# Decode-step kernel on one Trainium2 core: the prompt's latent attention gets its mask, identity and second queries one stage sooner, and the latent stage's last query stores are issued inside the attention

## What is computed

```
q_lat = einsum('bshd,chd->bshc', q[..., :QK_NOPE], w_uk)
def block(args):                                  # mla_prompt
    s = (einsum('bqhc,bkc->bhqk', ql, ckv) + einsum('bqhr,bkr->bhqk', qr, krope)) * MLA_SCALE
    p, _ = masked_softmax_stats(s, kpos[None, :] <= qpos[:, None])
    return einsum('bhqk,bkc->bqhc', p, ckv)
```

## Time and profile before

| what | value |
|---|---|
| median of three runs | 2103.25 us |
| profiled execution, first to last instruction | 2103.7 us |
| PE busy | 1934.1 us, 92% |
| DVE, ACT, POOL busy | 52%, 44%, 20% |
| latent stage and attention | about 638 to 1222 us of the span |
| the place of the change | 755 to 810 us of the span |

### The profile page before, as it was taken

How to read it: one execution, slowest core, us unless ns; L and a number is a source line. 1 busy time by engine, 2 the same in 40 slices (tenths; PEclk the granted TensorE clock), 3 DMA queues, 4 the chain that set the end, 5 groups by cost and what they waited for, 6 DMA issues and landing times. The chain is left out here.

```text
span 2103.7 us, 47545 instructions
## 1 busy us (share of the span) xinstructions
PE 1934.1 (92%) x17532; PEld 1475.6 (70%) x17532; DVE 1090.2 (52%) x3211; ACT 930.4 (44%) x2106; POOL 423.2 (20%) x583
## 2 busy tenths in 40 slices
PE   6999999788878968999999979999999989999997
PEld 5888888465656756676667746666666668888886
DVE  4423333377794437666767745555555753332232
ACT  4333332478772225556555534444444553333332
POOL 0111111234462213013310132222222210000000
PEclk9999999899999979999999989999999999999999
DMA  8333332443446451011200169977776462332231
GB/s 289 99 113 110 110 117 79 124 143 108 131 138 179 146 151 51 24 37 32 73 18 25 42 185 284 270 224 222 215 222 212 144 215 91 94 104 81 90 103 47
DMA packets 178428, 270.39 MB, mean 129 GB/s; under 512 B 28088, under 2 KB 138632, under 8 KB 169336
## 3 DMA queue, kind: packets, MB, share of 16 engines
q1 hardware_dynamic: 158456, 169.74, 28.5%
q0 software_dynamic: 19808, 98.40, 13.9%
HBM read 213.06 MB, written 54.76 MB: 127 GB/s over the span
## 5 line engine op out<-in xcount | busy, mean ns | idle before, releaser
L75 PE MATMUL proj_acc<-proj_w_hi,proj_x_hi 128*128 128x512 f32 (+2 forms) x544 | 197.5, 363 | 18.3 <-DVE proj_x_lo L299 12.6
L76 PE MATMUL proj_acc<-proj_w_lo,proj_x_hi 128*128 128x512 f32 (+2 forms) x544 | 196.0, 360 | 0.0
L77 PE MATMUL proj_acc<-proj_w_hi,proj_x_lo 128*128 128x512 f32 (+2 forms) x544 | 195.6, 360 | 0.0
L1614 ACT ACTIVATE mla_probs<-mla_probs,mla_bias 128x256 f32<-128x256 f32 (+15 forms) x128 | 152.6, 1196 | 22.3 <-DVEq L1678 13.2
L1671 DVE CUSTOM_DVE_ANT_0 mla_probs<-mla_scores,mla_zero 128x512 f32<-128x512 f32 x192 | 124.6, 686 | 64.8 <-PE mla_scores L1533 64.7
L1624 ACT ACTIVATE prompt_q_nope<-mla_turned 128x512 f32<-128x512 f32 x144 | 79.8, 597 | 163.7 <-PE mla_turned L1560 163.6
L1575 PE MATMUL mla_outs<-prompt_q_nope,prompt_val 128*64 128x256 f32 (+1 forms) x1152 | 136.2, 376 | 5.3 <-DVE prompt_q_nope L1688 3.9
L75 PEld LDWEIGHTS proj_acc<-proj_w_hi,proj_x_hi 128*128 128x128 f32 x544 | 104.0, 191 | 31.5 <-DVE proj_x_lo L299 12.6
L817 ACT ACTIVATE win_probs<-win_probs,win_bias 128x256 f32<-128x256 f32 (+1 forms) x256 | 117.4, 462 | 17.2 <-DVE win_bias L856 16.7
L1997 PE MATMUL dec_scores<-dec_keysT,sample_q_lat 128*64 128x512 f32 x512 | 123.0, 601 | 2.2 <-DVE dec_krT L2163 1.2
L353 DVE COPY proj_featT<-proj_tr 128x512 f32<-128x512 f32 x34 | 23.5, 692 | 188.1 <-PE proj_tr L406 186.4
(11 more groups left out here) (402 smaller groups left out, 4845.8 us busy)
## 6 DMA issues: line engine op xcount, KB each, us to landing
win_v_tile<-wv_out SPq DMA_DIRECT2D x75, 128.0 KB
proj_x_raw<-in_xT SPq DMA_DIRECT2D x17, 512.0 KB, 3.9
proj_rows<-in_x SPq DMA_DIRECT2D x17, 512.0 KB, 5.3
featT<-proj_featT POOLq DMA_DIRECT2D x34, 256.0 KB, 2.8
late_ckv<-in_xT SPq DMA_DIRECT2D x17, 512.0 KB, 6.8
host_buf<-mix SPq DMA_DIRECT2D x17, 512.0 KB, 3.6
late_ckv<-in_x SPq DMA_DIRECT2D x17, 512.0 KB, 4.1
y_out<-host_buf POOLq DMA_DIRECT2D x17, 512.0 KB, 6.5
```

Source lines behind the costliest of these rows:

```text
L75: pe.matmul(out, lh, rh, start=start, stop=False)
L76: pe.matmul(out, lh, rl, start=False, stop=False)
L77: return pe.matmul(out, ll, rh, start=False, stop=stop)
L1614: act.activation(row, row, ACT.Exp, bias=bias[:, at:at + 1], scale=-1.0, accum_out=total[:, at:at + 1]).then_inc(exp_done, 1)
```

## The change

Four edits. In the last chunk of the latent stage SP loads four more pieces ahead of the key store: the mask (256 KB, into the columns of `host_buf` that key chunk 3 will take later), the two parts of unit 1's queries, and the identity. After that store SP leaves the stage; the last stores of `q_rope` and `q_nope` are issued by SP inside the attention, `q_nope` between the loads of units 2 and 3, `q_rope` between key chunks 2 and 3. POOL copies the mask from `host_buf` to `mla_mask`, once, ahead of its first split. `probsT` lies in the memory of `k_nope` and its first write waits for `k_stored`.

```diff
@@ prompt_latent_projections, SP, last chunk
                     sp.dma_start(host.qr_raw[:, 0, :], io["mla_qr"][0:P, 0:host.CW]).then_inc(host.first_loaded, 16)
+                    sp.dma_start(host.mask_ahead, io["mla_mask"]).then_inc(host.mask_loaded, 16)
+                    sp.dma_start(host.qn_raw[:, 1, :], io["mla_qn"][0:P, host.CW:2 * host.CW]).then_inc(host.second_loaded, 16)
+                    sp.dma_start(host.qr_raw[:, 1, :], io["mla_qr"][0:P, host.CW:2 * host.CW]).then_inc(host.second_loaded, 16)
+                    sp.dma_start(host.ident, io["ident"]).then_inc(host.mask_loaded, 16)
                 sp.dma_start(io["mla_k"].rearrange("(g p) t -> p g t", p=P)[:, :, cols], k_nope[:]).then_inc(k_stored, 16)
                 if c + 1 < NCK:
                     load_cq(c + 1)
+                if c == NCK - 1:
+                    break
                 sp.wait_ge(roped, 2 * c + 2)
-                store_rope(sp, c, qr_stored if c < NCK - 1 else prompt.qr_last_stored)
+                prompt.store_rope(sp, io, c, qr_stored)
                 sp.wait_ge(act_kept, kept_on_act(c, PER - 1))
-                sp.dma_start(io["mla_qn"].rearrange("(g p) t -> p g t", p=P)[:, :, cols], q_nope[:]).then_inc(qn_stored, 16)
+                prompt.store_nope(sp, io, c)
@@ prompt_latent_attention
-        probsT = prompt.q_nope[:].rearrange("p (a b) t -> p a b t", a=2)
+        probsT = prompt.k_nope[:].rearrange("p (a b) t -> p a b t", a=2)
@@ SP
-            sp.dma_start(mask[:], io["mla_mask"]).then_inc(masks, 16)
-            sp.dma_start(ident, io["ident"]).then_inc(consts, 16)
-            load_q(1)
-            for c in range(1, SEQ // CH):
-                load_first_k(c)
+            load_first_k(1)
+            load_q(2)
+            prompt.store_nope(sp, io, SEQ // CH - 1)
+            load_q(3)
+            load_first_k(2)
+            prompt.store_rope(sp, io, SEQ // CH - 1, prompt.qr_last_stored)
+            sp.wait_ge(masks, 1)
+            load_first_k(3)
             for u in range(2, NU):
-                load_q(u)
+                if u > 3:
+                    load_q(u)
@@ POOL
+            pool.wait_ge(host.mask_loaded, 32)
+            pool.tensor_copy(mask[:], host.mask_ahead).then_inc(masks, 1)
@@ POOL, split_q
-                pool.wait_ge(q_loaded[u % 2], 32 * (u // 2 + u % 2))
+                if u == 1:
+                    pool.wait_ge(host.second_loaded, 32)
+                else:
+                    pool.wait_ge(q_loaded[u % 2], 32 * (u // 2))
@@ ACT and DVE, keep_turned
-                    dve.wait_ge(prompt.qn_stored, 16 * SEQ // CH)
+                    dve.wait_ge(prompt.k_stored, 16 * SEQ // CH)
@@ DVE
-            dve.wait_ge(masks, 16)
+            dve.wait_ge(masks, 1)
```

More of the change, by code:

```diff
@@ L465, in __init__ @@
         self.qn_raw, self.qr_raw = (self.buf[:, SEQ + 2 * k * self.CW:SEQ + 2 * (k + 1) * self.CW].rearrange("p (u t) -> p u t", u=2) for k in range(2))
-        self.first_loaded = b.sem("first_loaded")
+        self.mask_ahead = self.buf[:, SEQ - self.CH:SEQ]
+        self.first_loaded, self.second_loaded, self.mask_loaded = b.sem("first_loaded"), b.sem("second_loaded"), b.sem("mask_loaded")
 class LatentWeights:
@@ L923, in __init__, with store_rope, store_nope @@
         self.k_stored, self.qn_stored, self.qr_stored, self.qr_last_stored = (b.sem(n) for n in ("k_stored", "qn_stored", "qr_stored", "qr_last_stored"))
+    def store_rope(self, sp, io, c, done):
+        cols = slice(c * self.CH, (c + 1) * self.CH)
+        for g in range(2):
+            for d in range(2):
+                sp.dma_start(io["mla_qr"].rearrange("(g h d r) t -> g d h r t", g=2, d=2, r=ROPE)[g, d][:, :, cols], self.q_rope[:, g, :]).then_inc(done, 16)
+    def store_nope(self, sp, io, c):
+        cols = slice(c * self.CH, (c + 1) * self.CH)
+        sp.dma_start(io["mla_qn"].rearrange("(g p) t -> p g t", p=P)[:, :, cols], self.q_nope[:]).then_inc(self.qn_stored, 16)
 def prompt_latent_projections(nc, io, prompt, sample, ahead, host):
@@ L998, in kept_on_dve @@
             return c * DVE_PER + sum(ON_DVE[:i + 1])
[L1000 to L1004, removed]
         def kept_on_act(c, i):
@@ L1401, in prompt_latent_attention @@
         outs = b.ps("outs", [P, CH])
-        consts, k_loaded, q_loaded0, q_loaded1 = (b.sem(n) for n in ("consts", "k_loaded", "q_loaded0", "q_loaded1"))
+        k_loaded, q_loaded0, q_loaded1 = (b.sem(n) for n in ("k_loaded", "q_loaded0", "q_loaded1"))
         q_loaded = (q_loaded0, q_loaded1)
@@ L1545, in turn @@
                 if r == 0:
-                    pe.wait_ge(consts, 16)
+                    pe.wait_ge(host.mask_loaded, 32)
                 pe.wait_ge(exp_done, 2 * QB * (u + 1))
@@ L1619, in keep_turned @@
                 if g == 0:
-                    act.wait_ge(prompt.qn_stored, 16 * SEQ // CH)
+                    act.wait_ge(prompt.k_stored, 16 * SEQ // CH)
                 if g >= 2:
```

## The result

The changed kernel takes 2091.51 us in the median of nine runs (2088.77 to 2100.28), the kernel before 2103.25 (2096.22 to 2114.58). The ratio of the two is 0.9946, with a 95% interval of 0.9929 to 0.9962: 11.4 us less (0.0054 of 2103.25), 8.0 to 14.9 by the interval. The profiled execution went from 2103.7 to 2092.5 us, 11.2 us less.

The account below looks back on a forecast made before the run. PE, busy 92% of the span, leaves time only in idle holes and at its low clock. 3.75 + 7.5 + 0.9 + 0.5 - 0.1 = 12.55 us off the 2103.25 median gives 2090.7; 8-in-10 range 2087.5 to 2096.5.

Parts of the forecast that it names:

- the stage starts sooner: Change from latent stage to attention: SP leaves after the key store, ACT arrives last; 3.75 us won, bounds 0 and 3.75.
- the mask is there: Attention start: DVE takes the first scores 3.7 us into the stage instead of 11.18; 7.5 us won, bounds 7.2 to 7.6.
- POOL's share: Attention start: POOL's copy and split run while DVE splits; 0.1 us lost, bounds 0 and 0.9.
- the third hole: PE's 1.25 us wait for POOL's split of unit 1's queries mostly goes; 0.9 us won, bounds 0.5 and 1.25.
- the clock: First attention units: 0.7 us less at PE's low clock likely, half of it won; 0.5 us, bounds 0.1 and 1.7.
- The rival that the clock would not fall at all: Attention start: PE's shorter idle keeps its clock up; 3 to 4 us more won, 2087; chance 0.07.
- The moved transfers: Attention loads and stores on SP's queue, issued at new places: costed at nothing, each with a named cover.
- the thinnest place: Key chunk 2, issued behind the q_nope store, lands by 774 or 775, ACT wants it at 776.3; cover 1 to 2 us.
- The price of nothing: The moved transfers in the attention were costed at 0 us, as each was given cover.
- The rival of the late chunk: Attention: the q_nope store again takes 14.6 us, chunk 2 lands near 783; 6 us won, 2097; chance 0.12.

Follow-up runs that it names:

- the idle matmuls: Changed kernel with POOL's split of unit 1's queries held until DVE finishes unit 0's, plus ten unused 128x512 matmuls on PE at the attention's start; 2094.38 us, ratio 0.9956.
- the second profile of the changed kernel: Repeat of the changed kernel with nothing altered, measured against the kernel before; 2091.65 us, ratio 0.9948.
- the exchanged order: Changed kernel with the two late stores exchanged: q_rope between the loads of units 2 and 3, q_nope between key chunks 2 and 3; 2101.69 us, ratio 0.9996.
- the early loads alone: Changed kernel, but with the last query stores issued in the latent stage again and the early loads kept; 2108.23 us, ratio 1.0015.

## Why the prediction was right

The forecast of 2090.7 us stands 0.8 us from the measured median. That it is so near is in part luck: the sum was 1.0 us above the lead that the profile shows, and the interval of the measured gain is 8.0 to 14.9 us. Its steps, each against the changed kernel's profile:

| step | predicted | measured | from |
|---|---|---|---|
| the stage starts sooner | 3.75 | 3.9 | 767.90 to 763.81, less 0.2 of the stages ahead |
| the mask is there, less POOL's share | 7.4 | 6.6 | DVE's first scores 11.18 and 4.61 us into the stage |
| the third hole | 0.9 | 1.1 | first scores to those of unit 1, 5.18 and 4.10 us |
| the clock | 0.5 | 0.0 | from there to unit 0's output, 15.35 and 15.37 us |
| sum at unit 0's output | 12.55 | 11.5 | |

**The stage's start.** Right, and for the reason given: SP issued its eight DMAs in 0.34 to 0.43 us each and ACT, ending at 762.44, was the last.

**The mask.** The wait went as predicted, though the runs show that what it needed was only that nothing slow stood ahead of it; the early fetch that I priced as the means is worth 0.6 us at most in the profiles. The size was off by POOL's share: priced at 0.1 from the single overlap in the earlier trace rows, where a POOL cast lost 0.12, it cost 0.8. There I chose the row over the rule of the Trainium skill ("SBUF — State Buffer", section "SBUF: two separate sides"), which has such instructions shut each other out. By that rule the sum would have been some 0.5 us smaller, nearer to the measured one: the two DVE subtractions grew by 0.2 and 0.52 us, POOL's from 0.72 to 1.16. The trace agrees: DVE's two and POOL's one took 1.74 us together, from 765.13 to 766.87, and one after another they would take 0.68 + 0.42 + 0.72 = 1.82. The bound of 0.9 held it.

**The third hole.** Right within 0.2 us.

**The clock.** The fall came at 764.9 and the return at 775.1, with 10.2 us between them instead of 23.9:

```profile
764.00:765.00 1.00, 0.00 (x0) 0.00 (x0) 0.27 (x1) 1.00 (x3) 1.00 (x3) 0.94 0.13 41
775.00:776.00 1.00, 1.00 (x20) 0.81 (x16) 0.59 (x1) 0.00 (x1) 0.27 (x1) 0.94 0.38 135
```

Return sooner than forecast (776.5), and worth nothing. The step that failed is "PE is busy throughout that part, so half of it is won": PE's next scores need DVE to empty a buffer, and at the high clock PE waits 1.68 us at 779.28 where it waited 0.97 before. The same place after and before:

```profile
779.28 0.33 PE L1555 MATMUL mla_scores<-mla_k_hi,mla_qn_hi 64*128 64x128 f32 x1 [1.68 <-DVE mla_lowest L1693]
```

```profile
791.02 0.32 PE L1533 MATMUL mla_scores<-mla_k_hi,mla_qn_hi 64*128 64x128 f32 x1 [0.97 <-DVE mla_lowest L1671]
```

The rival that the clock would not fall at all was put at 3 to 4 us more by the same reasoning; the idle matmuls bought it for 1.4, with a wait for key chunk 2 that the forecast did not have. I did not see that the clock would fall again at unit 2, for 1.4 us. Falls of that kind go with most of the spread between runs of one kernel: of the 30 runs of the kernel before that stand beside the first experiments, the shortest took 2095.1 us at a mean granted clock of 0.978 and the longest 2113.7 at 0.965, and the correlation of the two over all 30 is -0.91.

**The moved transfers.** The cover held everywhere, but at the thinnest place only just. ACT split key chunk 2 without a wait at 776.49, and the chunk, issued at 769.93, had landed 6.4 us later, at 776.34: 0.15 us of cover where I had named 1 to 2. The price of nothing came true here with some luck; in the second profile of the changed kernel the cover was 1.0 us, and with the clock held up it was gone.

```profile
776.49 0.62 ACT L1630 ACTIVATE mla_k_hi<-host_buf 128x512 fp32r<-128x512 f32 x1
```

```profile
host_buf<-mla_k SPq DMA_DIRECT2D x1, 256.0 KB, 6.4
```

Unit 4's queries came late for POOL, as the row says, but its split was through at 789.5, 6 us ahead of PE's first score for that unit at 795.53:

```profile
787.38 0.40 POOL L1500 CAST mla_qn_hi<-host_buf 128x256 fp32r<-128x256 f32 x1 [9.52 <-DMA host_buf<-mla_qr]
```

**The rival of the late chunk** did not come true, but its price was too low. I had put it at 6.5 us and a time of 2097; the exchanged order, which brings it about, gives 2101.69 and a ratio of 0.9996. The wait itself was 6.95 us as worked out. What I left out is the clock, which falls again while PE stands still; that it takes the rest, some 3 us, is argued from the sizes and not shown by a run of its own.

## What to carry to other kernels

Behind the rotary stores the loads in the queue were late, small ones too (the identity's 64 KB took 9.3 us in the kernel before and 3.7 with the change): when a wait on a DMA is to go, look first at what stands ahead of it, and put what the next stage needs first ahead of the stores. Count the share of DMA engines that a transfer keeps busy; here a share near 4/16 belonged to an access whose outermost dimension was 4, and another cut of the same bytes was over twice as fast. A wait that is removed only shows its worth when the load behind it has cover too (the early loads alone won nothing), and work that is moved to run beside another engine's can slow that engine: POOL's split cost DVE's chain 0.8 us. Measure the cover of a moved transfer in the new profile even where no wait shows: here it was 0.15 us.

## What was not expected of the hardware

- The outermost dimension of a store's destination set its speed: 4 x 32 x 512 ran at 0.26 to 0.28 of the 16 DMA engines and 85 to 101 GB/s, 32 x 2 x 512 at 0.88 and 234 GB/s, for the same bytes.
- POOL and DVE, both reading two operands in SBUF, took 1.16 us in place of 0.72 and 0.94 in place of 0.42 when they ran side by side.
- The same instructions show a fall of PE's clock to 1.2 GHz in one profile and not in the next; in the window attention stage the time at the low clock ranged from some 19 to some 67 us, and the last rotary result behind it came at 754 to 770 us of the span. That is as much as the whole effect of this change, which is why the change needs medians and the leads of single instructions to be seen.
